# Three edits to a hybrid decoder step on one core: conditioning blocks round the second norm, x ahead of the weights, output turned block by block

## What is computed

```python
mod = silu(c) @ ada_w + ada_b                 # c: one row for the prompt, eight for the samples
sh1, sc1, g1, sh2, sc2, g2 = split(mod, 6)    # 2048 columns each
h = rms_norm(x) * (1 + sc1) + sh1
mix, states = token_mixer(h, ...)             # w_in, HGRN2 and mLSTM branches, gated merge, w_out
x = x + g1 * mix
h = rms_norm(x) * (1 + sc2) + sh2             # "the second norm"
up = h @ w_up                                 # 2048 -> 2 * 5632
y = (gelu(conv3(up[:, :5632])) * up[:, 5632:]) @ w_down
x = x + g2 * y
out = rms_norm(x, final_norm_w)               # "the last norm"
```

## Time and profile before

| | |
|---|---|
| median of 3 runs | 2337.15 us |
| the profiled execution's own time | 2335.63 us |
| its span, first to last instruction | 2333.9 us |
| PE busy | 2252.3 us, 97% |
| DVE, ACT, POOL busy | 1094.4, 1009.1, 326.4 us |
| mean granted TensorE clock | 0.984 |
| read from memory, written | 431.5 MB, 26.4 MB |

### The profile page before, as it was taken

The page is one execution under the profiler, slowest core; times in us unless marked ns, Lnnn a source line. Parts: engine busy times, 40 slices in busy tenths (PEclk is TensorE's granted clock), DMA queues, the critical chain, the costliest instruction groups (busy, mean ns, idle before and its releaser), DMA issues.

```text
span 2333.9 us, 42491 instructions
## 1 busy us (share of the span) xinstructions
PE 2252.3 (97%) x17440; PEld 2094.3 (90%) x17440; DVE 1094.4 (47%) x1433; ACT 1009.1 (43%) x1367; POOL 326.4 (14%) x452
## 2 busy tenths in 40 slices
PE   6889999999999999999999997999999999999997
PEld 3479999999999999898998986999999999999996
DVE  1235455455464444444444456455545555544443
ACT  4236454553554334443534435444444443433332
POOL 1010211211222212121111232000000000110000
PEclk9899999999999999999999998999999999999998
DMA  9967665666666576676665554666666655655552
GB/s 325 380 191 215 206 203 177 205 203 187 215 183 194 179 220 209 206 224 225 188 219 190 180 188 143 202 203 189 196 190 189 195 157 170 204 160 168 167 163 77
DMA packets 406624, 460.01 MB, mean 197 GB/s; under 512 B 14699, under 2 KB 379811, under 8 KB 405265
## 3 DMA queue, kind: packets, MB, share of 16 engines
q1 hardware_dynamic: 393856, 409.33, 55.7%
q0 software_dynamic: 11744, 46.03, 6.1%
q10 hardware_dynamic: 881, 2.57, 0.3%
HBM read 431.48 MB, written 26.39 MB: 196 GB/s over the span
## 4 chain that ended last, share of the span: by engine, by line
PE 92%; issue 3%; DMA 2%; ACT 1%; DVE 1%; POOL 0%; SPq 0%; POOLq 0%; ACTq 0%; DVEq 0%
PE ps L590 27%; PE ps L592 26%; PE ps L591 26%; PE ab L615 3%; PE R L569 2%; DMA uraw_x<-in_ada_w 1%; PE R L784 1%; PE R L811 1%; PE R L684 1%; DMA xT_spill<-xT 1%; DMA xtm<-in_x_sample 1%; PE ab L622 0%; PE R L765 0%; PE ab L701 0%; PE R L796 0%
## 5 line engine op out<-in xcount | busy, mean ns | idle before, releaser
L590 PE MATMUL ps<-xh,whi 128*128 128x288 f32 x3968 | 1200.6, 303 | 29.7 <-issue 12.7
L1384 DVE TENSOR_TENSOR wlo<-raw,whi 128x1024 fp32r<-128x1024 f32 x584 | 735.0, 1262 | 992.4 <-ACT whi L995 991.1
L592 PE MATMUL ps<-xh,wlo 128*128 128x288 f32 x3968 | 1174.8, 296 | 0.0
L591 PE MATMUL ps<-xl,whi 128*128 128x288 f32 x3968 | 1174.1, 296 | 0.0
L995 ACT ACTIVATE whi<-raw 128x1024 fp32r<-128x1024 f32 x584 | 615.5, 1057 | 819.5 <-PE ps L592 804.4
L590 PEld LDWEIGHTS ps<-xh,whi 128*128 128x128 f32 x3968 | 750.3, 189 | 94.8 <-issue 81.5
L591 PEld LDWEIGHTS ps<-xl,whi 128*128 128x128 f32 x3968 | 750.0, 189 | 0.0
L592 PEld LDWEIGHTS ps<-xh,wlo 128*128 128x128 f32 x3968 | 749.5, 189 | 0.0
L590 PE MATMUL ps<-ffh,whi 128*128 128x288 f32 x704 | 209.5, 298 | 0.0
L592 PE MATMUL ps<-ffh,wlo 128*128 128x288 f32 x704 | 207.5, 295 | 0.0
L591 PE MATMUL ps<-ffl,whi 128*128 128x288 f32 x704 | 207.2, 294 | 0.0
(11 more groups left out here) (365 smaller groups left out, 1609.5 us busy)
## 6 DMA issues: line engine op xcount, KB each, us to landing
raw<-in_w_in SPq DMA_DIRECT2D x288, 512.0 KB, 5.5
raw<-in_w_up SPq DMA_DIRECT2D x176, 512.0 KB, 3.8
araw<-in_ada_w SPq DMA_DIRECT2D x96, 512.0 KB, 4.8
raw<-in_w_down SPq DMA_DIRECT2D x88, 512.0 KB, 3.5
raw<-in_w_out SPq DMA_DIRECT2D x32, 512.0 KB, 3.4
araw_up<-in_ada_w SPq DMA_DIRECT2D x32, 512.0 KB, 4.6
uraw_x<-in_ada_w SPq DMA_DIRECT2D x30, 512.0 KB, 9.0
uraw<-in_ada_w SPq DMA_DIRECT2D x24, 512.0 KB, 7.1
```

Of the source, the lines that this page charges most:

```text
L590: mm(o, whi[:, s, kk, cols], hi[:, kt0 + kk, :], start=first and kk == 0, stop=False)
L591: mm(o, whi[:, s, kk, cols], lo[:, kt0 + kk, :], start=False, stop=False)
L592: x = mm(o, wlo[:, s, kk, cols], hi[:, kt0 + kk, :], start=False, stop=last and kk == KC - 1)
L1384: TT(wlo[:, s], raw[:, s], whi[:, s].bitcast(F32), ALU.subtract).then_inc(lo_done, 1)
```

## The change

**Second norm.** The last eight conditioning blocks leave the `w_up` loop (`UP_KINDS` has only "s") and run as eight *fills* of 16 matmuls from a ring of eight chunks, `afill`. In PE's order: fill 0 ahead of `w_out` chunk 4, fill 1 ahead of chunk 6, fills 2 and 3 after chunk 7, fills 4, 5 and 6 after the sum of squares, fill 7 ahead of `w_up` chunk 2. The turns of their rows come before chunks of the `w_out` stream (turn 0), after it (turn 1) and before `w_up` chunks 3 to 8 (turns 2 to 7). The `w_up` loop is sixteen chunks a time, the first time written out, then ten more. SP loads the ring among the first `w_up` chunks. POOL's spill of the new x moves behind three quarters of the second norm, and its clearing of `abuf` behind fill 7.

**Start.** SP issues x ahead of unit 0. Two tiles of x are turned before unit 0, the others two at a time. DVE adds the four groups of squares, and PE sums the result with 4 matmuls in unit 2. The last unit is turned before the rest of the early chunks; the last quarter of the norm is made in two halves. POOL's first spill waits for `u_used` 31 (the third pair of unit 7) in place of `lo_done` 7.

**End.** x comes back in blocks of two tiles (`x1b`, two buffers). After each `w_down` block DVE gates and adds in place and multiplies by the norm's weight (`yw`); after chunk 1 of the next block PE turns it (6 transposes, `tokens`), ACT evicts it into `ytm` after chunk 3, and DVE (not POOL) adds the squares after chunk 5. After the eighth block PE sums squares by token with six matmuls of three columns, ACT makes a root of 128 by 3 values, DVE its reciprocal, and ACT and DVE scale `ytm` in place; nine stores of 256 KB follow.

```diff
-UP_KINDS = "ssssssaa" * 2 + "ssss"
+UP_KINDS = "s" * 16
+FRING = 8
+FILL_P2 = {4: 0, 6: 1}
+FILL_UP = {2: 7}
...
+            for t in range(2):
+                sp.dma_start(xtm[:, t, :], x_prompt[0, P * t:P * (t + 1), :]).then_inc(ld_x, 16)
+            sp.dma_start(xtm[0:TS, 2, :], x_sample.rearrange("b t d -> (b t) d")).then_inc(ld_x, 16)
             for c in range(UC):
                 unit_load(0, c)
...
+            def fill_loads(*blocks):
+                for n in blocks:
+                    for e in range(4 * n, 4 * n + 4):
+                        if e >= FRING:
+                            sp.wait_ge(a_used, before_a(A_UP) + e - FRING + 1 + FREE)
+                        sp.dma_start(afill[:, e % FRING], ada_v[:, KC * (e % 4):KC * (e % 4 + 1), bass.ds(CN * (A_UP + n), CN)]).then_inc(u_landed[e // 2 % 4], 16)
...
+            def fill(n):
+                acc = fill_acc(n)
+                if n == 0:
+                    pe.wait_ge(ada_free, UNITS + A_UP - A_HG + FREE)
...
+                for c in range(4):
+                    e = 4 * n + c
+                    if c % 2 == 0:
+                        pe.wait_ge(u_landed[e // 2 % 4], 32 * (UNITS + e // FRING + 1))
+                    ada_chunk(afill[:, e % FRING], c == 0, c == 3, acc, KC * c).then_inc(a_used, 1)
...
                 unit(u, tiles)
+            unit_turn(UNITS - 1)
             drain(started)
-            unit_turn(UNITS - 1)
...
+            def p2_ahead(q):
+                if q == 6:
+                    fill_turn(0)
+                if q in FILL_P2:
+                    fill(FILL_P2[q])
+            stream(N_P2, "s" * 8, length=1, kt0=12, halves=XS + 4, ahead_of=p2_ahead)
+            fill_turn(1)
+            fill(2)
+            fill(3)
             pe.wait_ge(x1_acc, 3 + FREE)
...
+            for n in (4, 5, 6):
+                fill(n)
+
+            def up_ahead(q):
+                if q in FILL_UP:
+                    fill(FILL_UP[q])
+                if 3 <= q < 9:
+                    fill_turn(q - 1)
+            stream(up2_base(0), UP_KINDS, xparts=XS + 5, ahead_of=up_ahead)
...
                         chunk(down_base(i)[0] + k + 1, k, s == 0, s == 10, u % 2, ffh, ffl, KC * s, nothing())
+                        if s == 1 and 4 * i + u:
+                            tokens(4 * i + u - 1)
+                        if s == 7 and 4 * i + u == 7:
+                            pe.wait_ge(y_s, 7)
+                            token_squares(sqf, True)
...
+            def evict(b):
+                act.wait_ge(y_t, b + 1)
+                A(ytm[:, 0:2, 2 * P * b:2 * P * (b + 1)], R[:, 0, :].rearrange("p (t c) -> p t c", t=2), ACT.Copy).then_inc(y_c, 1)
+                A(ytm[0:TS, 2, 2 * P * b:2 * P * (b + 1)], sample_rows(b), ACT.Copy).then_inc(y_c, 1)
...
+            A(rsy[:, :], ab[:, 0:3], ACT.Sqrt, bias=epsc[:, 0:1], scale=1.0 / D).then_inc(rs_done, 1)
...
             pool.wait_ge(x_c, KT + X_FREE)
-            pool.wait_ge(lo_done, EARLY + 1)
+            pool.wait_ge(u_used, 4 * UNITS - 1)
```

379 lines of the change are left out of this document (231 added, 148 removed).

## The result

| | before | after |
|---|---|---|
| median | 2335.9 us (2334.37 to 2338.35, 4 runs) | 2310.41 us (2308.08 to 2315.46, 4 runs) |
| profiled execution | 2335.63 us | 2308.81 us |
| its span | 2333.9 us | 2306.9 us |

The ratio is 0.9892, 95% interval 0.9877 to 0.9906: 25.5 us gained where 42 were forecast, and 2310.4 lies outside the range of 2286 to 2305. Four more runs of the same kernel later had a median of 2307.58 us (ratio 0.9877, 0.9862 to 0.9892), outside the range too, so the miss is not one poor set of runs.

The account below looks back on a forecast made before the run. PE was taken as the bound, busy nine tenths or more almost throughout, with gains left at its gaps. Start 15.6, second norm 19.6 and end 7.5 made 42.7 us off 2335.63: 2292.9, named as 2294, range 2286 to 2305.

Parts of the forecast that it names:

- Ring of eight: Second norm: ring loads at 381 GB/s keep up with PE; fill 6 lands at about 1432, `w_up` starts at 1434.
- wrong if PE waits for `afill` loads: Second norm: a sign named beforehand that would show the prediction wrong, PE waiting for the ring's loads.
- Rival 2: Ring late once or twice, fill 6 or 0 delaying the stream; second norm gives 12 us, total 2302; chance 0.16.
- rival 4: Ring becomes a chain of latencies, every block from fill 2 on waiting a full round; slower, 2353 us; chance 0.03.
- The sum of squares: Second norm: its second half takes 2.1 us instead of 4.21 at half clock, on the path to the norm; 2.1 us gained.
- The loop: `w_up` loop: conditioning leaving saves 22.7 us; turns cost 3.8, fill 7 2.2 and waits 0.3; net 16.4 us.
- The start: Program start: loads 4.2, spill 9.7 and clock 1.7 give 15.6 us, between 9 and 20.
- The spill's term: Start: POOL's spill of x issued earlier moves the clearing and PE's bank forward by 9.7 us.
- The loads' term: Start: loads from 28 to 52 us run at 381 GB/s instead of 325; 4.2 us gained.
- Rival 1: Start gives half: spill lands late or PE stays at half clock; 7 us instead of 15.6, total 2303; chance 0.18.
- Up to the last update of C: Stretch from the first gate row to the last update of C: 0 us forecast.
- The end: `w_down` and tail: 6.3 us lost in the stream, 13.8 gained in the tail, net 7.5 us, between 4 and 9.

Follow-up runs that it names:

- Number 1: Changed kernel with the loads of fills 2 to 7 cut to half their bytes, so some values come out different; executed once, 2302.02 us.
- numbers 2: Changed kernel with ring loads in rows of 2 KB instead of 1 KB, as many bytes but other places of the weights; executed once, 2309.30 us.
- 8: Changed kernel with number 3's order, output rows 128 to 255 stored by ACT's queue, and 2 KB ring rows with the right weights; median 2300.97 us, ratio 0.9849.
- number 3: Changed kernel with PE's order altered: fill 2, four square-sum matmuls, fill 3, turn 1, the last four; median 2304.92 us, ratio 0.9881.
- number 4: Changed kernel with fill 6 moved from ahead of `w_up` to between its chunks 0 and 1; median 2309.86 us, ratio 0.9895.
- number 9: Changed kernel with POOL's spill of x at the start waiting again for the low part of a chunk after the norm; median 2319.29 us, ratio 0.9940.
- number 11: The changed kernel executed again with no edit; ACT's first gate row came at 162.40 us, 7.1 us ahead of before.
- number 6: Changed kernel with number 3's order, the new x stored behind the ring's last read, and output rows 128 to 255 stored by ACT's queue; median 2310.44 us.

## Why the prediction was wrong

- **Ring of eight: the failed step.** "Eight loads of 512 KB at 381 GB/s need 11 us ... fill 6, last ahead of `w_up`, lands at about 1432 against a start at 1434." The step took the ring block by block, with 4.6 us for a load to land, and never added up its bytes. Added up they leave no slack even at the forecast's own rate. In the clock of before (12.4 us later) SP starts on the ring at 1384.7, and 17.8 MB up to the last load of fill 6 take 47 us at 381 GB/s: 1431.5, the forecast's 1432. On top came 4.4 us for the 348 GB/s of its 1 KB rows, some 3 for 1.1 MB that was no piece of ring or `w_up`, and 2.5 for the pause behind turn 1: 1441.4. The last half of fill 6 ran at 1442.8, not by 1434, and a load took 8.3 us to land in the median. Fills 4 to 6 were costed at nothing, since they lie in PE's idle time; but it was their loads that had no room. Cost: 6.4 us for the start of `w_up`, of the 8.9 lost there. The forecast named the sign itself, "wrong if PE waits for `afill` loads"; it waited five times, 8.2 us. Number 1 shows the cause, numbers 2 and 8 the part of the rate, number 3 that of the pause, and number 4 that PE's order does not help. Rival 2 named this place and fill 6, and sized it at 7.6 us against 10 missed in the whole second norm; rival 4's chain of latencies did not come.
- **The sum of squares.** "Takes 2.1" was right for its second half (2.10) and beside the point. Turn 1 was held for 3.98 us by one `ada_block`, costed at 0.2 for DVE's time alone. The `ada_block` stands behind a chunk's low part and the adds of the product on DVE, and fills 2 and 3 and the first four square sums are queued behind the turn on PE. +2.1 was forecast, -2.0 came; number 3 gives 2.3 back.
- **The loop** was right: eight `w_up` chunks take 25.5 us; the five turns between the first and the second `abuf` cost (27.69 - 25.49) / 5 = 0.44 each instead of 0.63. 20.4 us against 19.2.
- **The start**, 15.6 forecast: 14.1 in the profiled execution and 12.0 over ten. The spill's term (9.7) is confirmed by number 9, with a wait of 9.12 us and a clearing 9.8 later. Chunk 8 stood behind no bank: PE worked through from 121.06 and the clearing came at 123.55, so PE decided, at about 127.4 (two chunks on) instead of 126. The loads' term of 4.2 was too large: unit 7's third pair came at 111.62 against 113.73, 2.1 us. The rate from 28 to 52 did rise as forecast (382 for 325), but from 4 to 12 us, with x on the same queue, it was 344 (413 before), and not in every execution did the rise come. So 14.1 beside 15.6 is partly luck: the mean of ten executions is 3.6 us short. Rival 1 ("or PE stays at half clock") describes the worse executions.
- **Up to the last update of C** nothing was forecast and 1.7 us were lost, 1.5 of them in one place by the clock (below). In number 11 the same stretch gained 1.4.
- **The end**: each `w_down` block takes 2113.03 - 2077.18 = 35.85 us, 35.8 forecast. The tail from the last square took 13.2 instead of 11.3. Eight of the stores' issues took 4.80 / 8 = 0.60 us each instead of 0.45 (in number 6 four took 1.88), but the first came earlier than forecast, so that the last stood 8.5 us behind the square where 8.3 was forecast, and number 6 shows that fewer of them help by half a microsecond. The step that failed here is "the last store needs 3.04 us from its issue": that was the last of a queue that had been half empty; here 2.4 MB land together, 4.7 us behind the last issue.

## What to carry to other kernels

Work moved into another engine's idle time brings its loads with it: add up all bytes that must land between the point where their memory is free and the point where they are needed, and divide by a rate measured with rows of the same length, with what is still on its way at the start and every pause for a slot on top. If that alone fills the time, no order of the waiting engine helps, and only fewer bytes, longer rows or an earlier start do (this case shows the first two). A wait that is cheap in itself must be priced by all that stands behind it in the queue of its engine, here one small turn with two fills and a sum of squares.
